# Second block's attention: probabilities normalised ahead of the turn, values stationary on column halves, outputs by features

## The chip, the cores and the metric

The kernel runs on one core of a Trainium2 chip. A core has TensorE (PE: products and transposes), VectorE (DVE), ScalarE (ACT), GpSimd (POOL) and SyncE (SP, which only issues transfers here). PEld is TensorE loading the stationary operand of a product. The metric is the time of one execution on the device in microseconds (us); smaller is better.

## What is computed

Two transformer blocks run one after the other, each of two layers, on one sequence of 256 positions and width 1024. The change is in the second block:

```python
for i in range(DEPTH):
    h = rms_norm_2(x, attn_norm_g[i])
    proj = h @ w_in[i]
    q, k, v, u, vv = jnp.split(proj, split_at, axis=-1)
    q = axial_rope(rms_norm_2(q.reshape(b, s, 8, 64), q_norm_g[i]), tables)
    k = axial_rope(rms_norm_2(k.reshape(b, s, 2, 64), k_norm_g[i]), tables)
    attn_o = gqa_attention(q, k, v)      # 8 query heads, 2 key/value heads, softmax over all 256 positions
    sg_o = spatial_gating(jax.nn.gelu(u), jax.nn.gelu(vv), ...)
    merged = jnp.concatenate([rms_norm_2(attn_o, attn_out_g[i]),
                              rms_norm_2(sg_o, sg_out_g[i])], axis=-1)
    x = x + merged @ w_o[i]
    ...
```

What is left out at the end is the feed-forward part with a depthwise convolution. Both RMS norms ahead of w_o are over 512 features of a position, so their roots can be applied behind the product with w_o, to each position's row.

## The kernel before

Every engine has its own program, written out by hand in one order; semaphores (counted up by one engine, waited for by another) tie them together. Inside an engine everything runs in the order of its program.

Large products are made in three parts: ScalarE rounds a weight piece (`raw` to `whi`, line 1168), VectorE takes the rest (`wlo`, line 1658), and TensorE multiplies high by high, high by low and low by high (lines 512 to 514, in `half`; one contraction step is those three). Weight pieces go through a ring of three `raw` and four `whi`/`wlo` buffers.

`proj` holds queries, keys, values, u and vv, with positions in the partitions (two halves `th`). Attention goes over four pairs of heads, g = 0 to 3; pair g is query head g with key/value head 0 and query head 4 + g with key/value head 1. For a pair TensorE turns the queries (`turn_queries`, line 958), VectorE copies them to `qk` (line 2184), and TensorE makes the scores in banks 3 and 4 (line 1033). VectorE takes the negated, scaled maxima (`negm`, lines 2210 and 2211). ScalarE makes the exponentials (`prob`, line 1541) with their sums in `rs`. TensorE turns them into bank 5 (`turn_weights(i)`, line 1016, one head at a time). ScalarE copies bank 5 to `probT` (`probs_out`, line 1288), and TensorE multiplies with the values into bank 7 (line 1052): the turned probabilities are the stationary operand, 128 columns of them at a time, and 64 columns of values move, eight products a pair.

The result has positions in the partitions. VectorE divides it by the sums into `proj` at column O2 (`heads_out`, lines 2188 and 2190). After pairs 1 and 3 TensorE turns two blocks of outputs (`turn_outputs`, line 1005), ScalarE and VectorE make `aTh` and `aTl` of them (lines 1301 and 1905), and ScalarE takes the sums of squares of whole rows (`out_squares`, line 1319). GpSimd makes the roots (lines 309 and 311), and VectorE adds the product with w_o times the root to x (line 1740).

Between these steps TensorE works on filler: `fill(g, n)` takes about 1000 columns' worth of steps from a list: the product for u (16 contraction steps, two a filler), the spatial mix `sg_mix` (line 975) and its turn `sg_turn` (line 987), then the half of w_o on the gated part (16 steps). What is left is done at the end, and then come the 16 steps on `aTh`. The other engines' `catch` evicts what the filler has finished: ScalarE's eviction of u (line 1224) is a gelu and needs another activation table than the exponentials, so a table is loaded ahead of it (line 1521) and behind it (line 1541). `split_to` splits weight pieces at set places.

## Time and profile before

| | us |
|---|---|
| median of 3 runs | 1459.55 |
| lowest, highest | 1459.24, 1459.56 |
| span of the profiled execution | 1458.2 |
| TensorE busy in it | 1438.4 |
| VectorE busy | 1038.7 |
| ScalarE busy | 810.0 |
| GpSimd busy | 64.8 |

The span is the time from the first to the last instruction in the profiled execution; a run's time is a little above it. "Busy" counts the time in which an engine has an instruction under way. Matmuls are pipelined and their ends are modelled, so the time that a group of them takes is best read from the start of one row to the start of the next. A float32 product shows as two instructions. In a timeline row stand the start, the time taken, the engine, the line, the operation, out<-in, the shapes and the count; in brackets the idle time before it and who ended it. A row of the windows has the stretch, its length, the busy time (and instructions) of PE, PEld, DVE, ACT and POOL, the granted clock of TensorE (1.00 is full), the transfers' share and GB/s. A row of the page's groups has the busy time, the mean ns of one, and after the second bar the idle time before them with what ended most of it.

### The profile page before, as it was taken

How to read it: one execution, taken by the hardware profiler on the slowest of the kernel's cores; microseconds unless marked ns; L12 is line 12 of the kernel's file. 1: busy time of each engine (PE TensorE's matmuls, PEld its weight loads, DVE VectorE, ACT ScalarE, POOL GpSimd, SP SyncE). 2: the span in 40 equal slices, each digit the busy share in tenths (PEclk: the TensorE clock that was granted, in tenths of full speed). 3: DMA queues.
4: the chain of work that ended last, by engine and by line, in shares of the span. 5: the costliest groups of instructions: out<-in, count | busy, mean ns of one | idle time of the engine just before them, and what ended most of it. 6: DMA issues, size and time to landing. Idle time of an engine off the chain costs nothing.

```text
span 1458.2 us, 19709 instructions
## 1 busy us (share of the span) xinstructions
PE 1438.4 (99%) x7731; PEld 1209.4 (83%) x7731; DVE 1038.7 (71%) x1417; ACT 810.0 (56%) x1159; POOL 64.8 (4%) x100
## 2 busy tenths in 40 slices
PE   6999999999999999999999999999999999999999
PEld 5888887888888788887888888788888888888888
DVE  5656885855557655885866556877988878788886
ACT  3556644444544555744354444677665567776563
POOL 2000000000000000000010000210000012000000
PEclk9999999999999999999999999999999999999999
DMA  8654643576565654552756655336566635456651
GB/s 297 214 181 142 223 144 127 168 237 191 175 206 197 201 161 155 189 173 87 226 182 223 202 186 193 125 110 219 166 191 201 224 123 171 129 181 199 200 186 58
DMA packets 172476, 261.08 MB, mean 179 GB/s; under 512 B 9312, under 2 KB 111360, under 8 KB 172128
## 3 DMA queue, kind: packets, MB, share of 16 engines
q1 hardware_dynamic: 170944, 254.13, 53.5%
q0 software_dynamic: 1152, 4.65, 1.0%
q8 instruction: 61, 1.00, 0.3%
q10 hardware_dynamic: 288, 1.05, 0.2%
q14 instruction: 31, 0.25, 0.0%
HBM read 256.65 MB, written 1.05 MB: 177 GB/s over the span
## 4 chain that ended last, share of the span: by engine, by line
PE 85%; DVE 8%; ACT 3%; issue 1%; POOL 1%; DMA 1%; SPq 0%; DVEq 0%; ACTq 0%
PE ps L441 16%; PE ps L512 10%; PE ps L514 10%; PE ps L513 10%; PE ps L442 9%; PE ps L411 6%; PE ps L415 6%; PE ps L413 6%; DVE wlo L1658 3%; PE ps L444 2%; ACT whi L1168 1%; PE ps L469 1%; DVE x L1677 1%; DVE x L1675 1%; DMA raw<-in_w_in 1%
## 5 line engine op out<-in xcount | busy, mean ns | idle before, releaser
L1658 DVE TENSOR_TENSOR wlo<-raw,whi 128x2048 fp32r<-128x2048 f32 (+1 forms) x238 | 528.5, 2230 | 224.1 <-ACT whi L1168 224.1
L1168 ACT ACTIVATE whi<-raw 128x2048 fp32r<-128x2048 f32 (+1 forms) x238 | 442.3, 1867 | 151.4 <-PE ps L514 54.3
L441 PE MATMUL ps<-xT,whi 128*128 128x512 f32 x1008 | 356.5, 395 | 0.0
L442 PE MATMUL ps<-xT,wlo 128*128 128x256 f32 x1152 | 311.2, 280 | 0.0
L512 PE MATMUL ps<-whi,xT 128*128 128x512 f32 (+3 forms) x640 | 250.5, 391 | 4.1 <-DVE xT L1684 1.6
L514 PE MATMUL ps<-whi,xT 128*128 128x512 f32 (+3 forms) x640 | 242.0, 378 | 0.0
L513 PE MATMUL ps<-wlo,xT 128*128 128x512 f32 (+3 forms) x640 | 241.4, 377 | 0.0
L441 PEld LDWEIGHTS ps<-xT,whi 128*128 128x128 f32 x1008 | 189.1, 188 | 42.3
L442 PEld LDWEIGHTS ps<-xT,wlo 128*128 128x128 f32 x1152 | 217.4, 189 | 6.1
L512 PEld LDWEIGHTS ps<-whi,xT 128*128 128x128 f32 x640 | 120.3, 188 | 27.6 <-issue 4.5
L514 PEld LDWEIGHTS ps<-whi,xT 128*128 128x128 f32 x640 | 120.2, 188 | 22.6
L513 PEld LDWEIGHTS ps<-wlo,xT 128*128 128x128 f32 x640 | 120.6, 188 | 18.9
L411 PE MATMUL ps<-whi,aTh 128*128 128x512 f32 x300 | 93.0, 391 | 0.0
L413 PE MATMUL ps<-wlo,aTh 128*128 128x512 f32 x300 | 92.7, 390 | 0.0
L415 PE MATMUL ps<-whi,aTl 128*128 128x512 f32 x300 | 92.6, 390 | 0.0
L2259 DVE SCALAR_TENSOR_TENSOR proj<-proj,rpb 128x255 f32<-128x255 f32 x160 | 70.1, 480 | 2.2 <-ACT proj L1580 0.7
L415 PEld LDWEIGHTS ps<-whi,aTl 128*128 128x128 f32 x300 | 56.3, 188 | 12.0
L413 PEld LDWEIGHTS ps<-wlo,aTh 128*128 128x128 f32 x300 | 56.3, 188 | 11.9
L411 PEld LDWEIGHTS ps<-whi,aTh 128*128 128x128 f32 x300 | 55.7, 188 | 10.3
L1457 ACT ACTIVATE prob<-ps 128x512 f32<-128x512 f32 x36 | 21.6, 600 | 72.4 <-PE ps L444 72.4
L444 PE MATMUL ps<-xT,whi 128*128 128x512 f32 x144 | 53.8, 396 | 0.0
L1580 ACT ACTIVATE proj<-proj,rpb 128x256 f32<-128x256 f32 x80 | 43.6, 593 | 13.6 <-DVE proj L2275 11.4
(236 smaller groups left out, 1943.7 us busy)
## 6 DMA issues: line engine op xcount, KB each, us to landing
raw<-in_w_in SPq DMA_DIRECT2D x124, 512.0 KB, 4.6
raw<-in_w_ffn_in SPq DMA_DIRECT2D x88, 512.0 KB, 4.9
raw<-in_w_up SPq DMA_DIRECT2D x88, 512.0 KB, 4.8
raw<-in_w_ffn_out SPq DMA_DIRECT2D x44, 512.0 KB, 4.4
raw<-in_w_down SPq DMA_DIRECT2D x44, 512.0 KB, 4.5
raw<-in_w_branch SPq DMA_DIRECT2D x24, 512.0 KB, 4.6
raw<-in_w_out SPq DMA_DIRECT2D x16, 512.0 KB, 4.3
raw<-in_w_o SPq DMA_DIRECT2D x16, 512.0 KB, 4.6
```

The lines of the kernel that those rows point to most:

```text
L411: PE.matmul(o, ah, hi[:, j, b], start=first and kt == 0, stop=False)
L413: PE.matmul(o, ah, lo[:, j, b], start=False, stop=False)
L415: mm = PE.matmul(o, al, hi[:, j, b], start=False, stop=last and j == c - 1 and i == len(kts) - 1)
L441: PE.matmul(ps[:, b, :], hi, m.xT[:, kt], start=kt == 0, stop=False)
L442: mm = PE.matmul(ps[:, b, 0:S], lo, m.xTh[:, kt], start=False, stop=False)
L444: mm = PE.matmul(ps[:, b, :], hi, m.xT[:, kt], start=False, stop=True)
L512: PE.matmul(o, ah, hi[:, j, :], start=kt == 0, stop=False)
L513: PE.matmul(o, ah, lo[:, j, :], start=False, stop=False)
L514: mm = PE.matmul(o, al, hi[:, j, :], start=False, stop=end)
L1168: AC.activation(m.whi[:, i % SPLIT, 0:w], m.raw[:, slot, 0:w], ACT.Copy).then_inc(s.w_hi, 1)
L1658: DV.tensor_tensor(m.wlo[:, i % SPLIT, 0:w], m.raw[:, slot, 0:w], m.whi[:, i % SPLIT, 0:w].bitcast(F32), ALU.subtract).then_inc(s.w_lo, 1)
L2259: a = DV.scalar_tensor_tensor(out=conv[:, f, to], in0=src[:, f, of], scalar=m.cw[:, c, f, tap:tap + 1], in1=conv[:, f, to], op0=ALU.mult, ...
```

## The change

Probabilities are now normalised before they are turned: VectorE multiplies `prob` by the reciprocal of the sums (`normalise_pair`, which the first block uses already), and the turn waits for that (`probs_in`) instead of the exponentials. In the product with the values the values are stationary (64 columns, one half of bank 7's partitions a head) and the turned probabilities move (256 columns), four products a pair. The result then has features in the partitions, as w_o's product needs it: `turn_outputs` is gone, ScalarE makes `aTh` and VectorE `aTl` from bank 7 directly. Since a pair's features are head g beside head 4 + g, the rows of w_o and the gains are loaded in that order (`load_pairs`, `pairs`). The squares are kept by features: ScalarE squares each pair, GpSimd adds the four, and two small products with a column of ones sum them over the partitions; VectorE copies the two columns to `small`. In each round of the loop the scores now come first, the turns behind them and the product last, and ScalarE's `probs_out` stands behind the exponentials.

```diff
+    def load_pairs(w, c0, width):
+
+        i = n["piece"]
+        slot = i % RING
+        dst = m.raw[:, slot, 0:4 * width].rearrange("p (k w) -> p k w", k=4)
+        SP.wait_ge(s.w_lo, i - RING + 1)
+        for j in range(2):
+            src = w[j * S:j * S + S, c0:c0 + width].rearrange("(k p) n -> p k n", p=64)
+            SP.dma_start(dst[64 * j:64 * j + 64], src).then_inc(k.raws[slot], 16)
+        n.up("piece")
...
-        for kts in ((4, 8), (0, 4)):
-            for j in range(2):
-                load_block(t["w_o_2"][L], kts, j * 512, 512)
+        for j in range(2):
+            load_block(t["w_o_2"][L], (4, 8), j * 512, 512)
+        for j in range(2):
+            load_pairs(t["w_o_2"][L], j * 512, 512)
...
+        for g in range(1, 4):
+            PO.wait_ge(s.o_squared, 4 * L + g + 1)
+            if g > 1:
+                PO.wait_ge(s.o_summed, n["summed"])
+            PO.tensor_tensor(o_squares(0), o_squares(0), o_squares(g), ALU.add).then_inc(s.o_summed, 1)
+            n.up("summed")
...
-        def turn_outputs(kts, b):
-
-            for i, kt in enumerate(kts):
-                for th in range(2):
-                    mm = PE.transpose(ps[:, b, i * S + th * P:i * S + (th + 1) * P],
-                                      m.proj[:, th, O2 + kt * P:O2 + (kt + 1) * P], m.ident[:])
-            mm.then_inc(s.o_turned, 1)
-
         def turn_weights(i):
 
-            PE.wait_ge(s.exped, h0 + i + 1)
+            PE.wait_ge(s.probs_in, p0 + i + 1)
             if i:
                 PE.wait_ge(s.probs_out, p0 + i)
             for kt in range(2):
@@ -1017,13 +1030,20 @@
                                       m.prob[:, i % 4, th, kt * P:(kt + 1) * P], m.ident[:])
             mm.then_inc(s.probs_turned, 1)
...
+        def mix_weights(g):
+
+            PE.wait_ge(s.probs_out, p0 + 2 * g + 2)
+            if m0 + g:
+                PE.wait_ge(s.pair_out, m0 + g)
+            for kt in range(2):
+                for j in range(2):
+                    mm = PE.matmul(ps[64 * j:64 * j + 64, 7, (g % 2) * S:(g % 2 + 1) * S],
+                                   m.proj[:, kt, 640 + 64 * j:704 + 64 * j], m.probT[:, j, kt * S:(kt + 1) * S],
+                                   start=kt == 0, stop=kt == 1)
+            mm.then_inc(s.pairs_mixed, 1)
+
         fill(0, 0)
         for g in range(5):
-            if g:
-                turn_weights(2 * g - 2)
-            fill(g, 1)
-            if g:
-                turn_weights(2 * g - 1)
             if g < 4:
                 PE.wait_ge(s.qk_out, g0 + g + 1)
                 PE.wait_ge(s.exped, h0 + 2 * g)
@@ -1036,34 +1056,29 @@
                             mm.then_inc(s.scored, 1)
             if g < 3:
                 turn_queries(g + 1).then_inc(s.qk_turned, 1)
-            if g == 3:
-                PE.wait_ge(s.pair_out, m0 + 2)
-                PE.wait_ge(s.qk_out, g0 + 4)
-                turn_outputs((0, 2), 6)
+            fill(g, 1)
+            if g:
+                turn_weights(2 * g - 2)
             fill(g, 2)
             if g:
-                PE.wait_ge(s.probs_out, p0 + 2 * g)
-                if g > 1:
-                    PE.wait_ge(s.pair_out, m0 + g - 1)
-                for th in range(2):
-                    for j in range(2):
-                        for kt in range(2):
-                            c = th * P + j * 64
-                            mm = PE.matmul(ps[:, 7, c:c + 64], m.probT[:, j, kt * S + th * P:kt * S + (th + 1) * P],
-                                           m.proj[:, kt, 640 + 64 * j:704 + 64 * j], start=kt == 0, stop=kt == 1)
-                mm.then_inc(s.pairs_mixed, 1)
+                turn_weights(2 * g - 1)
             fill(g, 3)
+            if g:
+                mix_weights(g - 1)
         fill(5, 0)
-        PE.wait_ge(s.pair_out, m0 + 4)
-        PE.wait_ge(s.probs_out, p0 + 8)
-        turn_outputs((1, 3), 5)
...
         def outputs_ready(th, kt):
-            if th == 0 and kt < 2:
-                PE.wait_ge(s.o_lo, 2 * L + kt + 1)
+            if th == 0:
+                PE.wait_ge(s.pair_out, m0 + kt + 1)
+            if (th, kt) == (0, 3):
+                PE.wait_ge(s.o_summed, 3 * L + 3)
+                for h in range(2):
+                    mm = PE.matmul(ps[:, 6, h:h + 1], m.gate[:, 0, 1152 + h * P:1152 + (h + 1) * P], m.ones[:, 0:1], start=True,
+                                   stop=True)
+                mm.then_inc(s.o_sum, 1)
...
-    def outputs_hi(kts, bank):
-        AC.wait_ge(s.o_turned, n.up("o_turned"))
-        for i, kt in enumerate(kts):
-            a = AC.activation(m.aTh[:, kt, :], ps[:, bank, i * S:(i + 1) * S], ACT.Copy, scale=m.pcol[:, kt:kt + 1])
-        a.then_inc(s.o_hi, 1)
+    def weighted_hi(m0, g):
+        AC.wait_ge(s.pairs_mixed, m0 + g + 1)
+        o = ps[:, 7, (g % 2) * S:(g % 2 + 1) * S]
+        AC.activation(m.gate[:, g // 2, 1152 + g % 2 * S:1152 + g % 2 * S + S], o, ACT.Square).then_inc(s.o_squared, 1)
+        AC.activation(m.aTh[:, g, :], o, ACT.Copy, scale=m.pcol[:, g:g + 1]).then_inc(s.pair_hi, 1)
...
-                probs_out(p0, 2 * g - 2, m0 + g - 1)
             if g == 2:
...
-                probs_out(p0, 2 * g - 1, m0 + g - 1)
             catch(2, L, "at", g, 1, ahead=0)
-            if g == 3:
-                catch(2, L, "at", 3, 2, ahead=0)
-            split_to(rounded[g])
             for j in range(2):
                 i, head = 2 * g + j, 4 * j + g
                 if g < 4:
...
-                outputs_hi((0, 2), 6)
-            else:
-                catch(2, L, "at", g, 2, ahead=0)
+            if g:
+                probs_out(p0, 2 * g - 2, m0 + g - 1)
+            split_to(rounded[g])
+            catch(2, L, "at", g, 2, ahead=0)
+            if g:
+                probs_out(p0, 2 * g - 1, m0 + g - 1)
             catch(2, L, "at", g, 3, ahead=0)
+            if g:
+                weighted_hi(m0, g - 1)
         catch(2, L, "at", 5, 0, ahead=0)
         split_to(s0 + 4)
-        outputs_hi((1, 3), 5)
-        out_squares(24, O2)
...
-    def outputs_lo(kts, bank):
-        DV.wait_ge(s.o_hi, n.up("o_hi"))
-        for i, kt in enumerate(kts):
-            a = DV.scalar_tensor_tensor(out=m.aTl[:, kt, :], in0=ps[:, bank, i * S:(i + 1) * S], scalar=m.pcol[:, kt:kt + 1],
-                                        in1=m.aTh[:, kt, :].bitcast(F32), op0=ALU.mult, op1=ALU.subtract)
-        a.then_inc(s.o_lo, 1)
-
+    def weighted_lo(g):
+        DV.wait_ge(s.pair_hi, n.up("pair_hi"))
+        DV.scalar_tensor_tensor(out=m.aTl[:, g, :], in0=ps[:, 7, (g % 2) * S:(g % 2 + 1) * S], scalar=m.pcol[:, g:g + 1],
+                                in1=m.aTh[:, g, :].bitcast(F32), op0=ALU.mult, op1=ALU.subtract).then_inc(s.pair_out, 1)
...
-        def heads_out(g):
-            DV.wait_ge(s.pairs_mixed, m0 + g + 1)
-            then(DV.reciprocal(m.ri[:, 2 * g:2 * g + 2, :], m.rs[:, 2 * g:2 * g + 2, :]))
-            for th in range(2):
-                a = DV.tensor_tensor(m.proj[:, th, O2:O2 + 512].rearrange("p (j g d) -> p j g d", j=2, g=4)[:, :, g, :],
-                                     ps[:, 7, th * P:(th + 1) * P].rearrange("p (j d) -> p j d", j=2),
-                                     m.ri[:, 2 * g:2 * g + 2, th].unsqueeze(2).broadcast_to([P, 2, 64]), ALU.mult)
-            a.then_inc(s.pair_out, 1)
...
-            if g == 3:
-                catch(2, L, "at", 3, 2, ahead=0)
-                outputs_lo((0, 2), 6)
             split_to(rounded[g])
-            if g != 3:
-                catch(2, L, "at", g, 2, ahead=0)
-            if g:
-                heads_out(g - 1)
+            catch(2, L, "at", g, 2, ahead=0)
+            if g < 4:
+                normalise_pair(h0, g)
             catch(2, L, "at", g, 3, ahead=0)
+            if g:
+                weighted_lo(g - 1)
         catch(2, L, "at", 5, 0, ahead=0)
         split_to(s0 + 4)
-        outputs_lo((1, 3), 5)
         catch(2, L, "at", 5, 1)
+        DV.wait_ge(s.o_sum, L + 1)
+        DV.tensor_copy(m.small[:, 24:26], ps[:, 6, 0:2]).then_inc(s.out_sq, 1)
```

In the piece of the order below TensorE is in the third round (g = 2). L1016 (L1029 after) turns the probabilities of one head, L1033 (L1053) makes scores, L958 turns queries, L975 (L996) is the spatial mix, L1052 (L1040) the product with the values. Before:

```order
L1016 MATMUL ps<-ident,prob 128x128 [waits probs_out,exped]
L1016 MATMUL ps<-ident,prob 128x128 x3
L1033 MATMUL ps<-qk 128x256 [waits exped,qk_out]
L1033 MATMUL ps<-qk 128x256 x3
L958 MATMUL ps<-ident,proj 128x128 [waits qk_out]
L958 MATMUL ps<-ident,proj 128x128
L975 MATMUL ps<-proj,rpb 128x128 [waits sg_in,free2]
L975 MATMUL ps<-proj,rpb 128x128 x3
L1052 MATMUL ps<-proj,probT 128x64 [waits pair_out,probs_out]
L1052 MATMUL ps<-proj,probT 128x64 x7
L975 MATMUL ps<-proj,rpb 128x128 [waits sg_in,free0]
L975 MATMUL ps<-proj,rpb 128x128 x3
```

After:

```order
L1029 MATMUL ps<-ident,prob 128x128 [waits probs_out,probs_in]
L1029 MATMUL ps<-ident,prob 128x128 x3
L996 MATMUL ps<-proj,rpb 128x128 [waits sg_in,free2]
L996 MATMUL ps<-proj,rpb 128x128 x3
L1029 MATMUL ps<-ident,prob 128x128 [waits probs_out,probs_in]
L1029 MATMUL ps<-ident,prob 128x128 x3
L996 MATMUL ps<-proj,rpb 128x128 [waits sg_in,free0]
L996 MATMUL ps<-proj,rpb 128x128 x3
L1040 MATMUL ps<-probT,proj 64x256 [waits pair_out,probs_out]
L1040 MATMUL ps<-probT,proj 64x256 x3
L1053 MATMUL ps<-qk 128x256 [waits exped,qk_out]
L1053 MATMUL ps<-qk 128x256 x3
```

The scores have moved from between to behind both turns and the product of the round before, and the product stands behind the second spatial mix.

ScalarE in the same round. L1288 (L1303) copies turned probabilities, L1224 (L1239) evicts u, L1541 (L1549) makes exponentials, L1316 and L1317 are the square and the copy of a pair. Before:

```order
L1288 ACTIVATE probT<-ps 128x512 [waits pairs_mixed,probs_turned]
L1521 ACT_TABLE_LOAD
L1521 ACTIVATE small<-half 128x1
L1288 ACTIVATE probT<-ps 128x512 [waits pairs_mixed,probs_turned]
L1224 ACTIVATE proj<-ps,small 128x512 [waits th0_sum]
L1224 ACTIVATE proj<-ps,small 128x512 [waits w_used]
L1541 ACT_TABLE_LOAD [waits probs_turned]
L1541 ACTIVATE prob,rs<-ps,negm,small 128x256 [waits negm]
L1541 ACTIVATE prob,rs<-ps,negm,small 128x256
L1541 ACTIVATE prob,rs<-ps,negm,small 128x256 [waits probs_turned,negm]
L1541 ACTIVATE prob,rs<-ps,negm,small 128x256
L1288 ACTIVATE probT<-ps 128x512 [waits pairs_mixed,probs_turned] x2
```

After:

```order
L1534 ACT_TABLE_LOAD
L1534 ACTIVATE small<-half 128x1
L1239 ACTIVATE proj<-ps,small 128x512 [waits th0_sum]
L1239 ACTIVATE proj<-ps,small 128x512 [waits w_used]
L1549 ACT_TABLE_LOAD [waits probs_turned]
L1549 ACTIVATE prob,rs<-ps,negm,small 128x256 [waits negm]
L1549 ACTIVATE prob,rs<-ps,negm,small 128x256
L1549 ACTIVATE prob,rs<-ps,negm,small 128x256 [waits probs_turned,negm]
L1549 ACTIVATE prob,rs<-ps,negm,small 128x256
L1303 ACTIVATE probT<-ps 128x512 [waits pairs_mixed,probs_turned] x2
```

Both copies of turned probabilities have moved behind the eviction of u, the table load and the four exponentials.

VectorE in the first and second round. L1658 (L1668) splits a weight piece, L2210 and L2211 are the maxima of the second pair, L2188 and L2190 were the division of the outputs, L1859 and L1863 are the normalising. Before:

```order
L1658 TENSOR_TENSOR wlo<-raw,whi 128x2048 [waits w_hi]
L2210 TENSOR_REDUCE negm<-ps 128x2 [waits scored]
L2211 SCALAR_TENSOR_TENSOR negm<-negm,small 128x2 [waits dve_step]
L2210 TENSOR_REDUCE negm<-ps 128x2 [waits scored]
L2211 SCALAR_TENSOR_TENSOR negm<-negm,small 128x2 [waits dve_step]
L2184 COPY qk<-ps 128x256 [waits qk_turned]
L1658 TENSOR_TENSOR wlo<-raw,whi 128x2048 [waits w_hi]
L2188 RECIPROCAL ri<-rs 128x4 [waits pairs_mixed]
L2190 TENSOR_TENSOR proj<-ps,ri 128x2x64 [waits dve_step]
L2190 TENSOR_TENSOR proj<-ps,ri 128x2x64
```

After:

```order
L1668 TENSOR_TENSOR wlo<-raw,whi 128x2048 [waits w_hi]
L1859 RECIPROCAL ri<-rs 128x4 [waits exped]
L1863 TENSOR_SCALAR prob<-prob,ri 128x256 [waits dve_step]
L1863 TENSOR_SCALAR prob<-prob,ri 128x256 x3
L2210 TENSOR_REDUCE negm<-ps 128x2 [waits scored]
L2211 SCALAR_TENSOR_TENSOR negm<-negm,small 128x2 [waits dve_step]
L2210 TENSOR_REDUCE negm<-ps 128x2 [waits scored]
L2211 SCALAR_TENSOR_TENSOR negm<-negm,small 128x2 [waits dve_step]
L2193 COPY qk<-ps 128x256 [waits qk_turned]
L1668 TENSOR_TENSOR wlo<-raw,whi 128x2048 [waits w_hi]
```

Normalising stands between the weight split and the maxima of the next pair.

## Rows read from the trace of the kernel before

**Rows 1.** The page: span, and each engine's busy time and instructions.

```profile
span 1458.2 us, 19709 instructions
...
PE 1438.4 (99%) x7731; PEld 1209.4 (83%) x7731; DVE 1038.7 (71%) x1417; ACT 810.0 (56%) x1159; POOL 64.8 (4%) x100
```

**Rows 2.** Windows: busy time of each engine, attention of both layers.

```profile
948.40:983.90 35.50, 35.16 (x234) 29.68 (x233) 26.50 (x57) 27.87 (x60) 4.00 (x4) 1.00 0.32 104
1218.30:1253.70 35.40, 35.06 (x234) 29.67 (x233) 26.51 (x57) 27.73 (x60) 4.00 (x4) 1.00 0.32 104
```

**Rows 3.** Timeline of TensorE, second round, first layer.

```profile
954.94 1.13 PE L1033 MATMUL ps<-qk 64*128 64x256 f32 x8
...
956.20 0.48 PE L512 MATMUL ps<-whi,xT 128*128 128x512 f32 x1
...
957.67 1.89 PE L1052 MATMUL ps<-proj,probT 128*128 128x64 f32 x16
959.37 0.48 PE L512 MATMUL ps<-whi,xT 128*128 128x512 f32 x1
```

**Rows 4.** Timeline of TensorE in the first block.

```profile
231.12 1.08 PE L626 MATMUL ps<-probT,proj 128*64 128x256 f32 x8
232.13 0.50 PE L512 MATMUL ps<-whi,xT 128*128 128x512 f32 x1
```

**Rows 5.** Timeline of TensorE, third round.

```profile
967.17 1.11 PE L975 MATMUL ps<-proj,rpb 128*128 128x128 f32 x8
...
968.11 0.60 PE L1016 MATMUL ps<-ident,prob 128*128 128x128 f32 x4
...
968.55 0.60 PE L987 MATMUL ps<-ident,proj 128*128 128x128 f32 x4
```

**Rows 6.** Timeline of VectorE: first block's normalising, then the second round.

```profile
638.46 1.14 DVE L1853 TENSOR_SCALAR prob<-prob,ri 128x256 f32<-128x256 f32 x4
...
955.70 2.28 DVE L1658 TENSOR_TENSOR wlo<-raw,whi 128x2048 fp32r<-128x2048 f32 x1
957.90 0.69 DVE L2210 TENSOR_REDUCE negm<-ps 128x2 f32<-128x512 f32 x1
```

**Rows 7.** ScalarE: third round's timeline; the page's group of weight splits.

```profile
963.98 1.26 ACT L1224 ACTIVATE proj<-ps,small 128x512 f32<-128x512 f32 x2
...
965.26 1.28 ACT L1541 ACT_TABLE_LOAD   x1
...
966.55 0.56 ACT L1541 ACTIVATE prob<-ps,negm,small 128x256 f32<-128x256 f32 x1
...
968.75 0.60 ACT L1288 ACTIVATE probT<-ps 128x512 f32<-128x512 f32 x1
...
970.65 0.83 ACT L1230 ACTIVATE bTh<-ps,pcol 128x256 fp32r<-128x256 f32 x2
...
L1168 ACT ACTIVATE whi<-raw 128x2048 fp32r<-128x2048 f32 (+1 forms) x238 | 442.3, 1867 | 151.4 <-PE ps L514 54.3
```

**Rows 8.** Timeline: the product on aTh, and the turn of x.

```profile
988.09 0.39 PE L512 MATMUL ps<-whi,aTh 128*128 128x512 f32 x1
...
988.96 4.48 DVE L1658 TENSOR_TENSOR wlo<-raw,whi 128x2048 fp32r<-128x2048 f32 x2
...
993.36 1.40 DVE L1740 SCALAR_TENSOR_TENSOR x<-ps,small,x 128x512 f32<-128x512 f32 x2
...
994.21 0.60 PE L469 MATMUL ps<-ident,x 128*128 128x128 f32 x4
```

**Rows 9.** Timeline: GpSimd's root and the addition to x.

```profile
977.84 0.19 POOL L309 TENSOR_SCALAR small<-small 128x2 f32<-128x2 f32 x1 [24.72 <-ACT gate L1319]
...
978.92 0.75 DVE L1740 SCALAR_TENSOR_TENSOR x<-ps,small,x 128x512 f32<-128x512 f32 x1 [1.40 <-POOL small L311]
```

**Rows 10.** Timeline of TensorE at the start.

```profile
8.57 2.18 PE L658 MATMUL ps<-ident 128*128 128x128 f32 x9 [8.57 <-DMA rope<-in_rope]
...
12.64 2.13 PE L658 MATMUL ps<-ident 128*128 128x128 f32 x18
```

19 lines of the change are left out of this document (11 added, 8 removed).

## The prediction

> **What bounds the kernel now.** I read the page's busy shares first: TensorE is busy for 1438.4 of 1458.2 us [rows 1], so a microsecond of its work that goes, or of waiting that comes, is a microsecond of the time. Then the windows of the second block's attention in both layers: in 35.5 us TensorE is idle 0.34 us [rows 2], while VectorE and ScalarE are busy for 26 to 28 us. Nothing waits here that matters; the reader is to see that TensorE's own work is all there is to save, and that the two other engines have only 8 us of slack a layer. Last I read the timeline row by row for what each step takes and which engine hands over to which.
>
> **What goes from TensorE.** One step is the time from one row's start to the next one's. The product with the values takes 959.37 - 957.67 = 1.70 us a pair [rows 3]. The new form (64 columns stationary, 256 moving) runs in the first block: 232.13 - 231.12 = 1.01 us [rows 4]. Saved: 0.69 x 4 = 2.8 us a layer. The two groups of four transposes of the outputs go too; four transposes take 968.55 - 968.11 = 0.44 us [rows 5], so 0.9. Together 3.7 us a layer, with the 0.34 idle at most 4.0.
>
> **What comes to other engines.** VectorE scales the probabilities: 1.14 us for four [rows 6] and some 0.2 for the reciprocal ahead of it, against a reciprocal and two narrow products before. ScalarE gets a square and a copy a pair and loses the squares of whole rows. Both have room for that; busy time is not the matter. GpSimd's three sums of 256 columns have no row like them: I bound one between 0.2 us (its narrow instruction) and three whole roots of 1.08, 3.2 us [rows 9], and take 1; the last may start 6 us before TensorE wants it, so it costs 0 at either bound. The 64-partition loads of w_o carry the same bytes and start a ring of three pieces ahead, so they cost 0; the cover is the 5 us that two splits take, and only a load later than that would cost its rest.
>
> **The order, which is what costs.** Each turn now waits for VectorE's normalising, and ScalarE makes the exponentials of the next pair ahead of its copy of the turned probabilities. The second turn of a pair waits for that copy, as its bank is one. So score, maxima, four exponentials and the copy stand in one chain beside only one or two filler steps. My steps: a filler of two contraction steps 957.67 - 956.20 = 1.47; scores with the next queries' turn 956.20 - 954.94 = 1.26 (scores alone 1.06); a turn 0.36 to 0.44; a spatial mix 968.11 - 967.17 = 0.94; its turn 0.44 [rows 3, 5]. Maxima may start when the scores end, 1.13 after their start [rows 3], and the first is ready 0.9 later (0.69 and its short follower, [rows 6]). Exponentials until the copy starts: 968.75 - 966.55 = 2.20; the copy 0.60 [rows 7].
>
> First layer, by clock of the old trace:
> - Turn 0. VectorE has its gated values and one weight split first, and is free at 957.90 as before [rows 6]. 0.2 for the reciprocal and 0.57 for the first head: 958.7. TensorE, whose first scores now come a filler earlier (it waits 0.35 there for exponentials 0), is there at 955.8. Wait 2.9.
> - Turn 1. TensorE there at 958.7 + 0.4 + 1.5 = 960.6. Normalising ends 957.9 + 0.2 + 1.14 = 959.2, maxima 960.1, exponentials 962.3, copy 962.9. Wait 2.3.
> - Mix 0 at 962.9 + 0.4 + 1.5 = 964.8. ScalarE splits a weight piece (1.9, [rows 7]) and copies 0.6: 965.4. Wait 0.6.
> - Turn 3. From 965.4: mix 1.0, scores and turn 1.3, the last filler of u 1.5: 969.2. ScalarE evicts u when that has ended (969.4), loads the table, makes the exponentials and starts the copy 968.75 - 963.98 = 4.77 after it began the eviction [rows 7]: 974.1, done 974.7. TensorE is there at 969.2 + 0.4 + 0.9 = 970.5. Wait 4.2. Before, both copies went ahead of this eviction.
> - Turn 5. From 974.7: turn, mix, product and scores end 978.1; then 0.44, turn 4 and 0.44: there at 979.4. ScalarE takes the turned gate (0.83, [rows 7]) from 978.75, exponentials 979.6 to 981.8, copy 982.4. Wait 3.0.
> - Mix 3 waits 0.3 behind a weight split.
>
> From turn 0 on TensorE's work up to the w_o product on aTh is 8 turns 3.1, 7 fillers 10.3, four products 4.3 with their small gaps, scores 2.4, mixes and turns of the gate 2.8, eight single steps 5.4: 28.3 us. With the waits 10.4 this ends at 958.7 + 28.3 + 10.4 = 997.4, against 988.09 [rows 8]: 9.3 us late. (By the other account: waits 0.35 + 2.9 + 10.4 = 13.7, less 4.0 saved: 9.7.)
>
> **Behind it.** The turn of x (L469) waited 0.2 us for VectorE, which adds to x right behind two splits that end 5.3 us after aTh's product begins [rows 8]. Now a copy of the sums (0.2) and GpSimd's root stand between them; root to VectorE is 978.92 - 977.84 = 1.08 [rows 9]. TensorE would be there some 0.3 later for the two small products, which the wait hides. Of these only the path counts: 5.3 + 0.2 + 0.1 + 1.1 + 0.75 = 7.5 instead of 6.12 us: 1.4 us more.
>
> **Sum.** 9.3 + 1.4 = 10.7 us a layer; the second layer has the same rows 269.8 us later [rows 2], so 21.4. The profiled execution's 1458.2 becomes 1479.6; the median of the runs is 1.35 above its span, so **1481 us**. The rest of the kernel is TensorE at its work and gives nothing back: its idle time is 20 us in all, 8.6 of them before the first product [rows 1, 10]. About 0.2% (3 us) is what a measurement here can tell from no change.
>
> **Rivals.**
> - *The clock.* At the start, after 8.57 us of nothing, nine small products take 2.18 us; 4.1 us later eighteen take 2.13 [rows 10], so TensorE first ran at half speed (1.2 of 2.4 GHz). The waits of 4.2 and 3.0 us, with thin work between, could bring that back. At half speed for up to 4.1 us it would lose up to 2 us each time, four times in all: 8 us, 1489. Against it: the granted clock is 1.00 in both windows [rows 2], and no wait of this size is there to go by. 15%. The Trainium skill ("TensorE: Matmul & The Clock Gate", section "Why this matters for your kernels") warns that the clock falls when TensorE is left idle between bursts of products; by it this change would be worse than my sum, and the start of the trace agrees with it.
> - *Table loads.* The load takes 1.28 us and the exponential starts 966.55, right behind its 965.26 [rows 7]. Were there a drain beside it of the load's own size, hidden before and now on the path, turn 3 would wait 1.3 longer in each layer: 1484. The trace has no room for it, as the eviction ends at 963.98 + 1.26 = 965.24. 3%. The Trainium skill's "ScalarE: Activation LUTs" (section "What ACT_TABLE_LOAD costs") names such a drain, with 2.66 us for a switch in all.
> - *Shallower waits.* If turn 0 waits 1 us and turns 3 and 5 half of what I find (VectorE and ScalarE doing in another order what they have ready), 5 to 6 us a layer go: 1470. Against it: both work strictly in the order of the program. 15%.
> - *Faster.* If the copy of the turned probabilities were ready when TensorE comes, only the saved work is left: 1459.5 - 8.0 + 2.8 = 1454. It decides at waits of 2.6 us a layer (4.0 saved less 1.4 lost). It asks that exponentials and copy (2.8) fit under one filler and a turn (1.9), with the eviction of u elsewhere. The rows are against it. 5%.
> - Waits that just balance the saving: 3%.
>
> **How the numbers follow.** Forecast 59%, in 1475 to 1486. The range goes down to shallower waits and up to the clock, 1469 to 1490; it leaves out the faster and the balanced case and about a third of those two. Faster 5%, the same 3%, slower 92%.
>
> **What would show it.** In the changed profile's waits, TensorE's turn of the probabilities waits for VectorE's prob once and for ScalarE's probT two or three times a layer, the longest 4 us in the third round behind the eviction of u. The product with the values takes 1.0 us in place of 1.7; TensorE's busy time falls by 5 to 8 us while the span grows. The window from the first scores to w_o's product is 9 to 10 us longer. The turn of x waits a microsecond for VectorE. Wrong would be: waits under 1 us in that round (order not as read), rows of the 512-column products longer than 0.40 behind a wait (the clock), or a difference outside these two windows.

## The result, and the profile after

The changed kernel takes **1486.17 us** (median of 4 runs, 1483.74 to 1486.95), the kernel before 1459.55 (1459.24 to 1459.8). The ratio is 1.018, with a 95% interval of 1.0169 to 1.0192: 26.6 us slower, 13.3 us a layer. The forecast was 1481, in a stated range of 1469 to 1490.

The page of the changed kernel, against [rows 1]:

```profile
span 1485.7 us, 19594 instructions
PE 1443.4 (97%) x7659; PEld 1203.0 (81%) x7659; DVE 1045.2 (70%) x1436; ACT 809.2 (54%) x1159; POOL 69.3 (5%) x106
PEclk9999999999999999999999999999999998999999
```

TensorE has less to do and yet is busy 5.0 us longer than before. Its waits say where it stands still (engine, line, whom it waited for: us in total, times, longest):

```profile
PE ps L1029 <- ACT probT L1303: 16.7, 6, 3.6
PE ps L1029 <- DVE prob L1863: 5.5, 2, 2.8
PE ps L490 <- DVE x L1750: 1.2, 2, 0.8
PE ps L1053 <- ACT prob L1549: 0.8, 2, 0.4
```

L1029 is the turn of the probabilities: 22.2 us of waits, where the whole kernel before had 0.7 us at its L1016. TensorE's timeline in the first layer shows them one by one (the last row is turn 3 of the second layer). The idle time in brackets begins at the modelled end of the row before, so it is some 0.2 us shorter than the delay from start to start. L1040 is the product with the values, L533 to L535 the products of 512 columns:

```profile
958.76 0.66 PE L1029 MATMUL ps<-ident,prob 128*128 128x128 f32 x4 [2.76 <-DVE prob L1863]
960.28 0.63 PE L534 MATMUL ps<-wlo,xT 128*128 128x512 f32 x1
962.98 1.09 PE L1029 MATMUL ps<-ident,prob 128*128 128x128 f32 x4 [1.65 <-ACT probT L1303]
975.56 0.63 PE L1029 MATMUL ps<-ident,prob 128*128 128x128 f32 x4 [3.63 <-ACT probT L1303]
977.01 1.08 PE L1040 MATMUL ps<-probT,proj 128*64 128x256 f32 x8
978.03 1.13 PE L1053 MATMUL ps<-qk 64*128 64x256 f32 x8
983.44 0.63 PE L1029 MATMUL ps<-ident,prob 128*128 128x128 f32 x4 [2.82 <-ACT probT L1303]
986.56 1.46 PE L1040 MATMUL ps<-probT,proj 128*64 128x256 f32 x8
999.92 0.50 PE L533 MATMUL ps<-whi,aTh 128*128 128x512 f32 x1
1007.19 0.65 PE L490 MATMUL ps<-ident,x 128*128 128x128 f32 x4 [0.35 <-DVE x L1750]
1258.20 1.09 PE L1029 MATMUL ps<-ident,prob 128*128 128x128 f32 x4 [3.63 <-ACT probT L1303]
```

The product itself is what was forecast, 978.03 - 977.01 = 1.02 us instead of 1.70. But the product on aTh starts at 999.92, not at 988.09 [rows 8]: 11.8 us late. And some rows are longer than they should be: L534 takes 0.63 us at 960.28, turn 1 takes 1.09, product 2 takes 1.46. The windows say why:

```profile
953.00:959.00 6.00, 3.14 (x18) 2.23 (x19) 5.79 (x10) 1.75 (x1) 0.11 (x1) 1.00 0.38 81
959.00:965.00 6.00, 4.35 (x17) 3.23 (x16) 2.42 (x7) 4.94 (x11) 0.00 (x0) 0.59 0.76 175
983.00:989.00 6.00, 5.56 (x23) 3.66 (x24) 2.25 (x8) 2.56 (x7) 0.00 (x0) 0.72 0.01 3
```

The granted clock fell from 1.00 to half, that is from 2.4 to 1.2 GHz, twice in the layer: from about 960.2 and from about 983.8. Both times TensorE had just waited 2.8 us. Before the first of these waits it had worked almost without a pause (busy 2.90 of the 3 us from 953 to 956); before the second it was busy for 5.99 of the 12 us from 971 to 983. Behind the longest wait of this layer, 3.63 us at turn 3, the clock stayed full. The second layer has waits as long or longer (turn 1 waits 2.18 us), but there the clock fell behind turn 1 (from about 1246.8) and behind turn 3 (its row above takes 1.09 us), and not behind the 2.82 us of turn 5. That makes four falls in the kernel.

### The profile page after: what moved, and what is told of

Same layout as the page of the kernel before. It is cut to its first block, busy times and chain, and to the rows that moved or that the text cites. A ratio compares the mean times of both kernels' runs of the same rounds, so it can differ in the third digit from the quotient of the medians.

```text
span 1485.7 us, 19594 instructions
## 1 busy us (share of the span) xinstructions
PE 1443.4 (97%) x7659; PEld 1203.0 (81%) x7659; DVE 1045.2 (70%) x1436; ACT 809.2 (54%) x1159; POOL 69.3 (5%) x106
## 4 chain that ended last, share of the span: by engine, by line
PE 82%; DVE 10%; ACT 3%; issue 2%; POOL 1%; DMA 1%; SPq 0%; DVEq 0%; ACTq 0%
PE ps L462 16%; PE ps L533 10%; PE ps L535 9%; PE ps L534 9%; PE ps L463 9%; PE ps L432 6%; PE ps L436 6%; PE ps L434 6%; DVE wlo L1668 3%; PE ps L465 2%; ACT whi L1183 1%; PE ps L490 1%; DVE x L1687 1%; DVE x L1685 1%; ACT prob L1549 1%
## 5 line engine op out<-in xcount | busy, mean ns | idle before, releaser
L1668 DVE TENSOR_TENSOR wlo<-raw,whi 128x2048 fp32r<-128x2048 f32 (+1 forms) x238 | 528.6, 2230 | 233.6 <-ACT whi L1183 233.6
L533 PE MATMUL ps<-whi,xT 128*128 128x512 f32 (+3 forms) x640 | 251.4, 393 | 2.8 <-DVE xT L1706 1.2
L535 PE MATMUL ps<-whi,xT 128*128 128x512 f32 (+3 forms) x640 | 243.1, 380 | 0.0
L534 PE MATMUL ps<-wlo,xT 128*128 128x512 f32 (+3 forms) x640 | 242.4, 379 | 0.0
L533 PEld LDWEIGHTS ps<-whi,xT 128*128 128x128 f32 x640 | 120.7, 189 | 26.4 <-issue 5.0
L535 PEld LDWEIGHTS ps<-whi,xT 128*128 128x128 f32 x640 | 120.8, 189 | 22.7
L534 PEld LDWEIGHTS ps<-wlo,xT 128*128 128x128 f32 x640 | 121.1, 189 | 19.0
L436 PEld LDWEIGHTS ps<-whi,aTl 128*128 128x128 f32 x300 | 56.3, 188 | 12.1
L434 PEld LDWEIGHTS ps<-wlo,aTh 128*128 128x128 f32 x300 | 56.3, 188 | 11.8
L432 PEld LDWEIGHTS ps<-whi,aTh 128*128 128x128 f32 x300 | 55.7, 188 | 10.3
```

What stands on the lines that cost most here:

```text
L432: PE.matmul(o, ah, hi[:, j, b], start=first and kt == 0, stop=False)
L434: PE.matmul(o, ah, lo[:, j, b], start=False, stop=False)
L436: mm = PE.matmul(o, al, hi[:, j, b], start=False, stop=last and j == c - 1 and i == len(kts) - 1)
L533: PE.matmul(o, ah, hi[:, j, :], start=kt == 0, stop=False)
L534: PE.matmul(o, ah, lo[:, j, :], start=False, stop=False)
L535: mm = PE.matmul(o, al, hi[:, j, :], start=False, stop=end)
```

## The experiments

All are compared with the kernel before, run on the same chip in the same sitting (1459.2 to 1459.4 us each time). "aTh" is the start of the product on aTh in the first layer, against 988.09 before; it comes from one profiled execution, while the times are medians. Line numbers shift a little from kernel to kernel.

| kernel | us | over before, a layer | aTh, later than before |
|---|---|---|---|
| the changed kernel | 1486.2 | 13.3 | 11.8 |
| old arithmetic in the new order | 1495.8 | 18.3 | 15.3 |
| new arithmetic in the old order | 1476.1 | 8.4 | 6.0 |
| the same, normalised by head | 1474.3 | 7.5 | 5.3 |
| changed, waits filled | 1479.2 | 9.9 | 8.5 |
| changed, no Gelu of u | 1482.7 | 11.7 | 11.7 |
| changed, copy first | 1488.1 | 14.4 | 13.1 |
| changed, values later | 1474.2 | 7.4 | 7.1 |
| moved, first try | 1483.6 | 12.1 | 6.2 |
| moved, second try | 1475.9 | 8.3 | 1.9 |
| moved, third try | 1458.6 | -0.3 | -1.7 |
| moved, fourth try | 1459.5 | 0.1 | -2.7 |

**The order alone.** The kernel before with its loops in the changed kernel's order, its arithmetic kept:

```diff
-            if g:
-                turn_weights(2 * g - 2)
-            fill(g, 1)
-            if g:
-                turn_weights(2 * g - 1)
             if g < 4:
...
+            fill(g, 1)
+            if g:
+                turn_weights(2 * g - 2)
```

> The kernel before with its own arithmetic (raw exponentials turned, products of 64 columns, the outputs turned by TensorE, one square per token) in the changed kernel's order: scores and query turn first, each turn a fill later, the product at the end of the round, ScalarE's copies behind the exponentials. Theory A (the waits come from the order): turn 0 has no wait, because it needs no normalised head; turn 1 waits about 3.8 us for the copy behind the exponentials (maxima after the split that ends at 957.9, then 0.9 + 2.2 + 0.6), turn 3 about 3.9 us, turn 5 about 2 us, some 9.7 us a layer: 1479 us, and 1484 us if TensorE's clock falls twice a layer as it did in the changed kernel. Rival B (the new arithmetic is what costs: sums on GpSimd, two small products, the longer way to the turn of x): within 1459 to 1464 us.

Measured: 1495.83 us (1492.05 to 1500.84), ratio 1.0262, interval 1.0234 to 1.0291. The turns' rows on TensorE:

```profile
962.20 1.09 PE L1016 MATMUL ps<-ident,prob 128*128 128x128 f32 x4 [3.90 <-ACT probT L1288]
975.10 0.85 PE L1016 MATMUL ps<-ident,prob 128*128 128x128 f32 x4 [3.64 <-ACT probT L1288]
985.33 0.84 PE L1016 MATMUL ps<-ident,prob 128*128 128x128 f32 x4 [2.39 <-ACT probT L1288]
```

The three waits are the expected 3.8, 3.9 and 2.0 us within 0.4. B falls: the old arithmetic in the new order is slower than the changed kernel. With the 0.40 us ahead of the second scores these waits are 10.3 us a layer, 20.5 in all, of the 32.7 us that the profiled execution (1492.05) lost. A's time, 1484 us at most, was too low by 8 to 17: two runs took 1492 us and two 1500. Behind all three waits the turn itself is long (0.84 to 1.09 us instead of 0.60), and the granted clock is 0.50 in 962 to 964, 976 to 978 and 986 to 988: three falls in the layer, where the changed kernel has two. The two longer runs have the lower mean clock (0.983 and 0.984, against 0.990 and 0.991). How much of the rest is the clock was not measured apart.

**The arithmetic alone.** The changed kernel with its loops put back into the old order:

```diff
             if g < 4:
                 PE.wait_ge(s.qk_out, g0 + g + 1)
...
             fill(g, 2)
+            if g:
+                mix_weights(g - 1)
+            fill(g, 3)
```

and `normalise_pair(h0, g)` on VectorE right behind `catch(2, L, "at", g, 1)`.

> The changed kernel's arithmetic in the order of the kernel before: each turn at the head of the round, scores after it, product ahead of the third fill; VectorE normalises a pair right behind its copy of the queries, ahead of the multiplications of the values and of the split. Theory A: the saving of 4.1 us a layer is there; waits of turn 0 about 1.2 us (exponentials end 952.96, then 0.17 + 0.57 + 0.3), turn 2 about 1.8, turn 4 about 2.1, turn 6 about 1.0 us, 6.1 us a layer, and 1.1 us for the turn of x: 1459.5 + 2 x (6.1 - 4.1 + 1.1) = 1466 us, range 1457 to 1471. Rival B (the arithmetic costs, in any order): 1478 us or more.

Measured: 1476.08 us (1474.29 to 1477.76), ratio 1.0115, interval 1.01 to 1.013. TensorE's waits for prob are 1.17, 1.34 and 2.07 us (expected 1.2, 1.8, 2.1) and none at turn 6. That is ten microseconds better than the changed kernel and ten worse than the expected 1466. Neither range holds: it lies above A's 1471 and 2 us under B's 1478, so by itself it doesn't decide between them. Its trace names what I had not counted: 1.0 us for the second half's multiplied values, which now stand behind the normalising on VectorE, up to 1.0 us for bTl, up to 2.2 us at the turn of x, and a half-clock stretch from 973.56. The normalisation does not fit the old order without delay either.

**By head.** The same, each head normalised as soon as its exponentials are there, and ScalarE's weight split moved behind the exponentials:

```diff
+                for j in range(2):
+                    i = 2 * g + j
+                    DV.wait_ge(s.exped, h0 + i + 1)
```

> As e1_sums_only (the changed arithmetic in the order of the kernel before), but each head is normalised by itself as soon as its exponentials are there, and ScalarE's weight split stands behind the exponentials. Theory A: turns 0, 2 and 4 wait 0.5, 0.9 and 0.7 us instead of 1.17, 1.34 and 2.07, the wait of 1.0 us for the multiplied values of the second half stays, the clock stays full: 3 us a layer under e1_sums_only, 1470 us, range 1467 to 1472. Rival H (the normalisation costs VectorE's time and not its delay, so that finer pieces bring nothing): 1475 to 1478 us.

Measured: 1474.31 us (1472.67 to 1474.71), ratio 1.0101, interval 1.0086 to 1.0116. Neither range holds. Turn 0's wait is gone, turns 1 and 3 now wait 0.57 and 1.21 us for ScalarE's copy, since its weight split now stands ahead of it; and the wait for the multiplied values grew to 1.56 us:

```profile
PE ps L1029 <- ACT probT L1303: 3.6, 4, 1.2
PE ps L1008 <- DVE proj L1731: 3.1, 2, 1.6
PE ps L1029 <- DVE prob L2223: 2.8, 2, 1.4
```

**The clock by itself.** The changed kernel, with identity products that nothing reads put into the waits:

```diff
+        def spin(g, n):
+
+            PE.wait_ge(s.pair_out, m0 + g - 1)
+            for i in range(n):
+                PE.transpose(ps[:, 7, (g - 1) % 2 * S + i % 2 * P:(g - 1) % 2 * S + (i % 2 + 1) * P], m.ident[:], m.ident[:])
...
+            if g == 1:
+                spin(g, 20)
...
+            if 0 < g < 4:
+                spin(g, (0, 12, 24, 20)[g])
```

> The changed kernel, with identity products that nothing reads put on TensorE into the waits of turns 0, 1, 3 and 5 (20, 12, 24 and 20 of them, some 0.1 us each), shorter than the waits at full clock. Theory A: nothing else moves, the granted clock stays at 1.00 in the windows where it was 0.59 and 0.72, the rows of 512 columns take 0.40 us there and not 0.63, and the time falls by 4 to 5 us: 1481 to 1482 us, as was forecast without the clock. Rival C (the half clock lay inside waits and cost nothing): 1486 us. Rival D (it cost as much as the prediction's rival said, 8 us): 1478 us.

Measured: 1479.17 us (1479.12 to 1479.47), ratio 1.0137, interval 1.0122 to 1.0152; 7.0 us under the changed kernel. The same two windows as above:

```profile
959.00:965.00 6.00, 4.95 (x32) 3.82 (x32) 2.41 (x6) 5.07 (x11) 0.00 (x0) 1.00 0.85 175
983.00:989.00 6.00, 6.00 (x35) 4.37 (x34) 2.66 (x8) 4.18 (x8) 1.93 (x4) 1.00 0.00 0
```

The granted clock is 1.00 in both, and 1.000 on the mean of the whole run (0.993 in the changed kernel). The first turn still starts at 958.51 (958.76 in the changed kernel): the waits are as long, only filled. So the half clock costs 7 us here, 1.7 a fall, nearly what rival D said and more than my 4 to 5; C falls. A kernel with 152 more products is faster, and what differs is the clock.

**The chain of the third round.** The changed kernel with u copied and its Gelu left out, so that ScalarE loads no table there:

```diff
-            if g == 2:
-                AC.activation(m.small[:, 60:61], m.half[:, 0:1], ACT.Gelu_apprx_tanh)
...
-                AC.activation(m.proj[:, half, U2:U2 + 512], ps[:, bank, :], ACT.Gelu_apprx_tanh,
+                AC.activation(m.proj[:, half, U2:U2 + 512], ps[:, bank, :], ACT.Copy,
```

> The changed kernel; u of the second block is copied and its Gelu is left out, so that ScalarE loads no table in the third round (two loads of 1.28 us fewer between the fill's end and the exponentials). Theory A (the chain eviction, load, exponentials, copy sets the wait of turn 3): the wait of 3.63 us falls by 1.3 to 2.6 us and the time by 2.6 to 5.2 us: 1481 to 1483.5 us. Rival E (the first load and the eviction lie beside a wait for something else, scores or maxima): the wait stays within 0.3 us and so does the time, 1486 us.

Measured: 1482.70 us (1479.03 to 1486.05), ratio 1.016, interval 1.0136 to 1.0185. ScalarE and TensorE:

```profile
970.29 0.69 ACT L1239 ACTIVATE proj<-ps,small 128x512 f32<-128x512 f32 x1 [1.48 <-PE ps L535]
973.80 0.93 PE L1029 MATMUL ps<-ident,prob 128*128 128x128 f32 x4 [2.21 <-ACT probT L1303]
```

Turn 3's wait falls from 3.63 to 2.21 us, within A's range; only the second load was on the path, since the eviction now waits for the fill (1.48 us). In this trace the clock fell three times in the first layer, once right behind the shorter wait (0.93 us for the turn), and took back what was won: aTh starts only 0.1 us earlier. The runs fall in two groups, 1486.0 us twice (the profiled one is of these) and 1479.0 and 1479.4, so the median lies in A's range where no run is. E falls by the wait, and A holds for it; for the time the runs don't decide.

**The copy's place.** The changed kernel with the even head's copy ahead of everything else of ScalarE's round:

```diff
         for g in range(5):
+            if g:
+                probs_out(p0, 2 * g - 2, m0 + g - 1)
             if g == 2:
...
-            if g:
-                probs_out(p0, 2 * g - 2, m0 + g - 1)
             split_to(rounded[g])
```

> The changed kernel with one move on ScalarE: the copy of the even head (probs_out of 2g-2) stands ahead of the third round's table preload, of the evictions and of the exponentials, not behind them. Theory A (what limits a round is the whole chain on ScalarE, eviction, table, exponentials and two copies, up to the next product and the next scores, not the one wait): the waits of turns 1, 3 and 5 for probT vanish (1.65, 3.63, 2.82 us), but products 0 and 1 wait for the odd head's copy instead (about 2.6 and 4.5 us) and the scores of pair 3 wait for exponentials; the time stays within 3 us of the changed kernel's, 1483 to 1489 us. Rival F (the copy's place behind the exponentials is itself the cost): the waits go and nothing takes their place, 10 us fewer, 1474 to 1478 us.

Measured: 1488.06 us (1487.41 to 1488.69), ratio 1.0197, interval 1.0182 to 1.0212. The waits moved to the products, as A said they would. Turn 1 and turn 3 wait for nothing, turn 5 for 0.34 us; instead, in the waits of both layers:

```profile
PE ps L1040 <- ACT probT L1303: 13.7, 8, 3.5
```

and in the timeline, at product 1:

```profile
976.78 1.97 PE L1040 MATMUL ps<-probT,proj 128*64 128x256 f32 x8 [3.52 <-ACT probT L1303]
```

Product 0 waits 1.11 us, less than the expected 2.6, and product 1 3.52 instead of 4.5; a spatial mix waits 1.37 for the eviction of u, and the scores of pair 3 for nothing. The time is in A's range, and F falls. A wait named at a turn is only where the chain shows: with one copy moved, it shows elsewhere.

**VectorE's order.** The changed kernel, the values multiplied in round 1 and pair 0 normalised at once:

```diff
-            if g == 0:
+            if g == 1:
                 DV.wait_ge(s.vv_root, L + 1)
...
-            split_to(rounded[g])
             catch(2, L, "at", g, 2, ahead=0)
             if g < 4:
                 normalise_pair(h0, g)
+            if g:
+                split_to(rounded[g])
```

> The changed kernel with VectorE's order alone moved: pair 0 is normalised right behind the fill's catch of round 0, the multiplications of the second half's values (4 of them, about 2.6 us) go to round 1 behind its maxima, and the weight splits behind the normalisation. Theory A (the first round's waits, 2.76 and 1.65 us, are VectorE's queue and nothing else): turn 0 waits for nothing, turn 1 at most 0.5 us, product 0 about 0.6 us; the first half-clock stretch goes too; 5 to 6 us a layer, 1475 us, range 1473 to 1478. Rival G (turn 1 waits for ScalarE's exponentials whatever VectorE does, and VectorE's moved work delays the maxima of round 2): 1 to 3 us a layer, 1480 to 1484 us.

Measured: 1474.16 us (1473.39 to 1475.45), ratio 1.0103, interval 1.0087 to 1.0118. This is A to the point: turn 0 without a wait, turn 1 waits 0.27 and product 0 0.19 us, and 12 us of the 26.6 are gone by VectorE's order alone. The first stretch at half clock is gone, but turn 3 still waits 3.63 us, and now the clock falls behind it:

```profile
969.34 1.09 PE L1029 MATMUL ps<-ident,prob 128*128 128x128 f32 x4 [3.63 <-ACT probT L1303]
```

**Everything moved.** Four tries to give the new arithmetic an order with short chains. The first: one fill step more ahead of the first scores, so that u ends in round 1 and its table load and eviction stand there; the even head's copy between the two heads' exponentials; the weight splits at the ends of the rounds.

```diff
-        fill(0, 0)
+        fill(0, 0, share=2000)
...
+                if g and not j:
+                    probs_out(p0, 2 * g - 2, m0 + g - 1)
...
+            if g == 1:
+                AC.activation(m.small[:, 60:61], m.half[:, 0:1], ACT.Gelu_apprx_tanh)
```

> The changed kernel's arithmetic and TensorE's order, with what surrounds it moved to where the chains are free: one more piece of the fill ahead of the first scores, so that u ends a fill earlier and its table preload and eviction stand at the end of round 1; the even head's copy between the two heads' exponentials; VectorE's order as in e7_values_later; weight splits behind the round's copies. Theory A (all the loss is chains at wrong places, the arithmetic itself saves 4 us a layer): no turn waits over 0.5 us, product 1 about 0.7 us, granted clock 1.00 throughout the stage, 1454 us, range 1450 to 1458, below the kernel before. Rival I (the arithmetic saves nothing in the end, since the small products, the sums on GpSimd and the later eviction of x give it back): 1459 to 1464 us even without waits.

Measured: 1483.58 us (1482.59 to 1484.86), ratio 1.0169, interval 1.0152 to 1.0186. Both ranges are missed. Rounds 0 and 1 ran without a wait, but in round 1 VectorE's split stood behind ScalarE's late one, and the maxima of pair 2 behind both (4 us late; turn 3 waited 5.06 us, and the clock fell behind it). And splits that come late free their buffers late, so that a load comes late, and at the end the turn of x waits for it all:

```profile
997.91 1.92 ACT L1183 ACTIVATE whi<-raw 128x2048 fp32r<-128x2048 f32 x1 [3.36 <-DMA raw<-in_w_up]
1004.19 0.66 PE L490 MATMUL ps<-ident,x 128*128 128x128 f32 x4 [3.09 <-DVE x L1753]
```

The second try put the splits early again and gave the multiplications of the values to GpSimd:

```diff
+            a = PO.tensor_tensor(v, v, root_v[:, th, :].unsqueeze(2).broadcast_to([P, 8, 64]), ALU.mult)
```

> As e9_moved, mended by what its trace showed (VectorE reached the maxima of rounds 2 and 3 about 4 us late, behind a weight split; a late split put off a load and with it the turn of x): both weight splits of the first rounds stand early, the first ahead of the normalisation of pair 0, the second in round 1; the second half's values are multiplied by GpSimd, which is idle there; the table preload stands behind round 1's exponentials; in round 3 both copies stand ahead of the odd head's exponentials. Theory A (the loss is chains at wrong places, the arithmetic saves 4 us a layer): turn 3 and products 1 and 2 wait under 1 us each, the granted clock is 1.00, 1454 us, range 1451 to 1460. Rival I (the arithmetic saves nothing in the end): 1460 to 1464 us without a wait over 0.5 us at a turn. Rival J (GpSimd's multiplications take over 9 us or slow VectorE beside them, so that the second half's mix waits): 1462 to 1475 us.

Measured: 1475.93 us (1473.92 to 1476.17), ratio 1.0109, interval 1.0093 to 1.0126. GpSimd was quick enough, and turn 3 and products 1 and 2 wait under 0.5 us, but in round 1 (VectorE and GpSimd):

```profile
953.97 4.64 DVE L1881 TENSOR_SCALAR prob<-prob,ri 128x256 f32<-128x256 f32 x4
953.08 2.71 POOL L394 TENSOR_TENSOR proj<-proj,small 128x512 f32<-128x512 f32 x2
955.87 2.58 POOL L399 TENSOR_TENSOR proj<-proj,rpb 128x512 f32<-128x512 f32 x2
```

The four rows that take 1.14 us [rows 6] took 4.64 and ended together with GpSimd's work. That made turn 1 wait 2.65 us. Behind the stage another 6.4 us a layer were lost: the third split had slipped behind a copy, ScalarE waited 3.27 us for the load behind it, and the copy of the sums stood behind VectorE's split of that piece. The turn of x waited 3.00 us in the first layer and 4.48 in the second, and the clock fell there too (granted 0.50 from 1001 to 1004). The time is above all three ranges, J's by 0.9 us.

The third try: values back to VectorE in round 1, splits of VectorE in rounds 0, 3 and 4, sums copied one split earlier.

```diff
+            if g in (0, 3, 4):
+                split_to((s0 + 1, 0, 0, s0 + 2, s0 + 3)[g])
...
-        catch(2, L, "at", 5, 1)
+        catch(2, L, "at", 5, 1, ahead=SPLIT - 1)
         DV.wait_ge(s.o_sum, L + 1)
```

> As e10_all_moved, mended by its trace: the second half's values are multiplied by VectorE again, in round 1 (beside GpSimd's multiplications VectorE's normalisation of pair 0 took 4.64 us and not 1.14); VectorE rounds the second weight piece in round 3 and both engines round the third at the start of round 4; the sums of squares are copied ahead of the weight split that waits for a load. Theory A (the arithmetic saves 4 us a layer, and chains at wrong places were the whole loss): no wait of a turn or a product over 1 us, about 2 us of waits a layer, the turn of x waits under 0.6 us, granted clock 1.00: 1455 us, range 1452 to 1461. Rival I (the arithmetic saves nothing): 1461 to 1466 us with the same waits. Rival K (the weight loads set the pace behind the stage, so that what the stage gains is lost ahead of the turn of x): the stage from the first scores to the product with w_o is under 38.5 us and the time still 1459 us or more.

Measured: **1458.57 us** (1458.41 to 1458.91, 11 runs), before 1459.22 (15 runs), ratio 0.9995, interval 0.9986 to 1.0004: no difference from the kernel before. The page, the waits of the turns, and two rows of TensorE:

```profile
span 1457.5 us, 19594 instructions
PE 1433.8 (98%) x7659; PEld 1198.0 (82%) x7659; DVE 1044.0 (72%) x1436; ACT 808.8 (55%) x1159; POOL 69.4 (5%) x106
```

```profile
PE ps L1029 <- ACT probT L1303: 2.1, 2, 1.1
```

```profile
986.43 0.39 PE L533 MATMUL ps<-whi,aTh 128*128 128x512 f32 x1
994.94 0.66 PE L490 MATMUL ps<-ident,x 128*128 128x128 f32 x4 [0.58 <-DVE x L1754]
```

aTh starts 1.66 us earlier than before, with waits of 1.06, 0.42 and 0.50 us (turn 3, product 1, bTl) still in it. From start to start these are about 2.5 us together, and the one of the kernel before, which is gone, was 0.50: the arithmetic takes 3.6 to 3.7 us of TensorE's work out of the layer up to aTh. TensorE's busy time is 4.6 us below [rows 1]. But the second turn of x starts at 994.94 against 995.36, only 0.42 earlier.

The time is in A's range, 3.6 us above its figure, and below I's. K's stage is there (986.43 - 948.50 = 37.9 us, under its 38.5), its 1459 us is missed by 0.4, and its cause is not in the trace: ScalarE waits 1.47 us for the load of w_up, but has rounded that piece at 990.05, and VectorE comes to it only at 991.94. What gives the gain back is what I names, the sums' longer way to x: from aTh to the second turn of x it is 8.51 us, 7.27 before, and that 1.2 us is the changed kernel's too.

The fourth try takes three of the remaining waits away:

```diff
-        catch(2, L, "at", 5, 1, ahead=SPLIT - 1)
+        catch(2, L, "at", 5, 1, ahead=SPLIT - 2)
```

```diff
+            if g == 1:
+                AC.activation(m.small[:, 60:61], m.half[:, 0:1], ACT.Gelu_apprx_tanh)
             catch(2, L, "at", g, 2, ahead=0)
...
+            catch(2, L, "at", g, 1, ahead=0)
             if g == 3:
                 probs_out(p0, 4, m0 + 2)
-            catch(2, L, "at", g, 1, ahead=0)
```

> As e11_best with three small moves read from its trace: the sums of squares are copied one weight split earlier (the second turn of x waited 0.58 us for VectorE), the second half's turned values are copied ahead of the turned weights in round 3 (a fill waited 0.50 us for bTl), and the Gelu table is loaded ahead of round 1's last copy (turn 3 waited 1.06 us for the chain behind it). Theory A: each wait goes by 0.3 to 0.6 us and nothing takes its place, 1.0 to 1.5 us a layer: 1456 us, range 1455 to 1457.5. Rival L (each of the three waits hides another that ends as late, as in the copy-first kernel): 1458 to 1459 us, no change from e11_best.

Measured: 1459.50 us (1459.24 to 1461.01, 11 runs), ratio 1.0004, interval 0.9995 to 1.0013. The waits of turn 3 and bTl are nearly gone (0.33 us and none), product 0 now waits 0.56, and aTh comes another 1.0 us earlier. All of it is lost at the second turn of x:

```profile
987.16 1.92 ACT L1183 ACTIVATE whi<-raw 128x2048 fp32r<-128x2048 f32 x1 [1.46 <-DMA raw<-in_w_up]
988.02 0.16 DVE L2242 COPY small<-ps 128x2 f32<-128x2 f32 x1 [1.12 <-PE ps L1079]
988.54 0.70 POOL L323 TENSOR_TENSOR small<-small,half 128x2 f32<-128x2 f32 x1
989.34 0.75 DVE L1754 SCALAR_TENSOR_TENSOR x<-ps,small,x 128x512 f32<-128x512 f32 x1 [1.16 <-POOL small L323]
990.01 4.48 DVE L1672 TENSOR_TENSOR wlo<-raw,whi 128x2048 fp32r<-128x2048 f32 x2
994.41 0.74 DVE L1754 SCALAR_TENSOR_TENSOR x<-ps,small,x 128x512 f32<-128x512 f32 x1
995.21 0.66 PE L490 MATMUL ps<-ident,x 128*128 128x128 f32 x4 [1.83 <-DVE x L1754]
```

The chain is that of the sums and of VectorE's order: the small products (L1079), their copy, GpSimd's root, the first addition to x, two splits, the second addition, TensorE. The load of w_up is not in it: ScalarE has rounded that piece at 989.08, before VectorE's splits begin at 990.01. A falls. L holds in that nothing is gained, though not in its detail (two of the three waits did go) nor quite in its time: 1459.50 is 0.5 above its range. With the copy of the sums earlier, both splits come between the two additions, where the third try had one.

**GpSimd beside VectorE.** The kernel before with the same multiplications on GpSimd:

```diff
-            if g == 0:
-                DV.wait_ge(s.vv_root, L + 1)
...
+        PO.wait_ge(s.vv_root, L + 1)
...
+            a = PO.tensor_tensor(v, v, m.brow[:, 128:640], ALU.mult)
+        a.then_inc(s.sg_in, 1)
```

> The kernel before with one move: the second half's values are multiplied by GpSimd instead of VectorE. It asks what VectorE's 4.64 us instead of 1.14 us for four TENSOR_SCALAR rows came from. Theory M (whatever VectorE does beside GpSimd's TENSOR_TENSOR is slowed): the weight split, 2.28 us alone, takes 4 us or more beside them and GpSimd's own rows stay at about 1.3 us each; the maxima of pair 1 are no earlier. Theory N (only the TENSOR_SCALAR kind is slowed): the split stays at 2.3 us, the maxima of pair 1 start about 3 us earlier. In both the time is within 0.2% of before, 1457 to 1461 us, since TensorE waits for neither.

Measured: 1459.29 us (10 runs, 1459.14 to 1459.73), ratio 1.0, interval 0.9991 to 1.0009. The split took its usual 2.28 us, but it had begun at 951.35, ahead of GpSimd's rows, and overlapped them only from 952.87 to 953.6, so it does not tell M from N. The maxima start at 955.77, 2.1 us earlier than before. Of VectorE's rows beside GpSimd's (which run from 952.87 to 958.14) three show what is slowed:

```profile
955.77 0.69 DVE L2221 TENSOR_REDUCE negm<-ps 128x2 f32<-128x512 f32 x1 [2.14 <-PE ps L1044]
956.50 0.43 DVE L2222 SCALAR_TENSOR_TENSOR negm<-negm,small 128x2 f32<-128x2 f32 x1
957.56 0.60 DVE L2222 SCALAR_TENSOR_TENSOR negm<-negm,small 128x2 f32<-128x2 f32 x1
```

The reduction out of PSUM keeps its 0.69 us. The tiny operation with two operands in SBUF, 0.16 us elsewhere, takes 0.43 and 0.60. So not all of VectorE is slowed, and not TENSOR_SCALAR alone: M and N both fall.

## Why the prediction was right, and where not

**Direction and cause: right.** The change saves TensorE's work and pays with waits of the turns for chains that the order made longer. The order alone costs more than the whole change, and with another order the same arithmetic costs nothing, nor does it gain anything that can be told from the noise.

**The waits: right one by one.** Forecast and found in the first layer: turn 0 2.9 and 2.76 us; turn 1 2.3 and 1.65 (at half speed the fill ahead of it covers more; the filled kernel has 2.3 us there, 12 products of 1.47 us and 0.87 of rest, and the second layer, where the clock is still full, 2.18); turn 3 4.2 and 3.63; turn 5 3.0 and 2.82; the second scores 0.35 and 0.38. The two I had at 0.6 and 0.3 (product 0, product 3) are not there; with the waits filled, product 0 waits 0.18. The reasons were right as far as they were tested: moving VectorE's multiplications removed the first two, and taking the table loads away shortened the third. Turn 5's was not tested by itself.

**The step that failed: the clock at no cost.** It was the rival that I gave 15%, at up to 2 us a time, four times, 8 us. It came, four times, for 7.0 us, measured by filling the waits. Without it the changed kernel takes 1479.2 us, 1.8 under the forecast of 1481; with it 1486.2, just above the 1475 to 1486 that I gave the forecast itself. The stated range holds only because it was drawn up to the clock. My reason against it was that the granted clock is 1.00 in both windows [rows 2]; but before, TensorE was idle there for only 0.34 us, so they could not speak on it. I expected it behind the waits of 4.2 and 3.0 us; in the first layer it came behind turn 0 and turn 5. The sign that I named for it, rows of 512 columns longer than 0.40 us, is there (0.63 at 960.28). The Trainium skill's warning ("TensorE: Matmul & The Clock Gate", "Why this matters for your kernels") names idle gaps between bursts of products as what brings the clock down. The trace agrees with that, but the length of a gap alone doesn't sort the cases: in the first layer the clock fell behind 2.76 and 2.82 us and not behind 3.63.

**The saving: right.** 3.7 us a layer of work forecast, 3.6 to 3.7 found in the third moved kernel. TensorE's busy time was to fall by 5 to 8 us; it rose by 5.0, with rows at half speed longer, and is 4.6 lower where the clock is full. The two small products (0.36 us a layer) count in it.

**The product on aTh: 9.3 us late forecast, 11.8 found, 8.5 without the clock.** The remaining 0.8 is the waits that were over-estimated.

**Behind it: right.** The turn of x comes 7.27 us after aTh begins, forecast 7.5. (The 0.2 us that I had it wait before was a misreading: its row at 994.21 starts a step after the one ahead of it, without idle time.) VectorE's rows are the path as described, two splits, the copy of the sums, and the addition behind GpSimd's root:

```profile
1000.67 4.48 DVE L1668 TENSOR_TENSOR wlo<-raw,whi 128x2048 fp32r<-128x2048 f32 x2
1005.08 0.15 DVE L2236 COPY small<-ps 128x2 f32<-128x2 f32 x1
1006.38 1.41 DVE L1750 SCALAR_TENSOR_TENSOR x<-ps,small,x 128x512 f32<-128x512 f32 x2 [1.16 <-PE ps L535]
```

It costs 1.2 us a layer (second turn of x 8.46 us after aTh begins, 7.27 before), forecast 1.4. The loads of w_o, which I put at 0, cost 0: ScalarE waits for none of them in the changed kernel. What I had not seen is that this 1.2 us stays when the stage gets shorter, and that in the moved kernels it and the two splits take most of the gain.

**The table load: rival refuted.** ScalarE's rows in the third round:

```profile
970.00 1.33 ACT L1239 ACTIVATE proj<-ps,small 128x512 f32<-128x512 f32 x2
971.34 1.28 ACT L1549 ACT_TABLE_LOAD   x1
972.64 0.56 ACT L1549 ACTIVATE prob<-ps,negm,small 128x256 f32<-128x256 f32 x1
```

The load starts when the eviction ends and the exponential 1.30 us later. The Trainium skill ("ScalarE: Activation LUTs", "What ACT_TABLE_LOAD costs") has a drain of about 1.38 us beside the load; this trace has no room for it.

**Shallower waits and faster: refuted** for this order, with the waits above, and both engines did what stands next in the program.

## What to carry to other kernels

Where two engines hand work back and forth, write down everything that the slower one does from one hand-over to the next; a wait moves along that chain when one item is moved, and only a shorter chain shortens it. On a kernel that keeps TensorE busy, put a price on new waits beyond their length: here two of the four long waits of a layer brought a stretch at half speed, 1.7 us each. Measure that part by filling the waits with products that nothing reads. A saving inside one stage is real only if what the next stage waits for comes earlier too; here that was the addition to x, behind two splits and GpSimd's root.

## What the hardware showed unexpectedly

- A wait's length alone does not say whether the clock falls. Behind the same 3.63 us at turn 3, the changed kernel's turn takes 0.63 us in the first layer (full clock) and 1.09 in the second (half), and that of the kernel with the values later 1.09. Behind the same 2.76 us at turn 0 the changed kernel runs 1.2 us more at full clock, and the kernel with the copy first none (its turn takes 1.11 us). What decides between them stays open.
- VectorE's TENSOR_SCALAR on fp32 in SBUF took 4.64 us for four beside GpSimd's TENSOR_TENSOR, 1.14 alone. The Trainium skill ("SBUF — State Buffer", "Who interferes with whom") says that beside a VectorE instruction in a mode with two ports, which `tensor_scalar` can enter, the engine that comes second "fully blocks"; which mode these rows ran in, no trace shows. It also says that a VectorE instruction with two inputs in SBUF contends with a GpSimd instruction that reads SBUF, and that `tensor_reduce` does not contend. The rows agree: the four end within 0.2 us of GpSimd's last, the small operation with two SBUF inputs goes from 0.16 us to as much as 0.60, and the reduction from PSUM stays at 0.69.
